# Fourth up unit of each MLP by seven quarter products, and x scaled by g and b on GpSimd

## What is computed

```python
def sq_relu_mlp(h, w_up, w_down):
    return jnp.square(jax.nn.relu(h @ w_up)) @ w_down
...
    xl = layer_norm(ALPHA * xl + ml[2] * dl, p["ln1_g"], p["ln1_b"])
    fl = sq_relu_mlp(modulate(xl, ml[3], ml[4]), p["w_up"], p["w_down"])
    xl = layer_norm(ALPHA * xl + ml[5] * fl, p["ln2_g"], p["ln2_b"])
```

## Time and profile before

| | |
|---|---|
| median of 3 runs | 1445.81 us (1445.0 to 1446.02) |
| span of the profiled execution, first to last instruction | 1442.8 us |
| difference of that span to the median | 3.0 us |
| TensorE busy | 1397.0 us, 97% of the span |
| VectorE busy | 1040.2 us, 72% |
| ScalarE busy | 543.1 us, 38% |
| GpSimd busy | 77.3 us, 5% |
| chain that ended last | TensorE 79%, VectorE 10%, ScalarE 5% |

### The profile page before, as it was taken

One profiled execution on the slowest core, in us unless ns is written; L12 is line 12 of the kernel. 1 busy time (PEld: TensorE's weight loads), 2 busy tenths in 40 slices (PEclk: granted clock), 3 DMA queues, 4 the chain that ended last, 5 costly groups with the idle time before them and its releaser, 6 DMA issues.

```text
span 1442.8 us, 22837 instructions
## 1 busy us (share of the span) xinstructions
PE 1397.0 (97%) x8806; PEld 1240.1 (86%) x8806; DVE 1040.2 (72%) x1651; ACT 543.1 (38%) x982; POOL 77.3 (5%) x146
## 2 busy tenths in 40 slices
PE   4999999999999999999999999999999999999996
PEld 3899988766779998998899879888999889989985
DVE  3694566777568876776776796877887677667778
ACT  4333343367454332332232254434443223223322
POOL 1300000010201000000000111001000000000011
PEclk9999999999999999999999999999999999999998
DMA  9701234696713312321221723551332122123141
GB/s 316 232 30 60 88 118 133 213 310 228 265 45 137 126 59 83 94 87 59 87 88 58 268 88 114 185 185 37 146 103 85 62 88 88 59 87 116 59 160 73
DMA packets 132300, 177.47 MB, mean 123 GB/s; under 512 B 4170, under 2 KB 104258, under 8 KB 131698
## 3 DMA queue, kind: packets, MB, share of 16 engines
q1 hardware_dynamic: 123250, 146.46, 31.4%
q0 software_dynamic: 7376, 26.76, 5.3%
q10 hardware_dynamic: 1584, 3.01, 0.6%
HBM read 166.94 MB, written 9.27 MB: 122 GB/s over the span
## 4 chain that ended last, share of the span: by engine, by line
PE 79%; DVE 10%; ACT 5%; issue 2%; DMA 2%; SPq 1%; POOL 0%; ACTq 0%; DVEq 0%
PE ps L801 40%; PE ps L1325 20%; PE ps L783 5%; PE ps L792 4%; PE ps L832 2%; DVE convT L2024 2%; PE ps L1133 2%; DVE wlo L1926 1%; ACT h_full L1722 1%; SPq L570 1%; DVE p_pad L2691 1%; DMA raw_more<-in_w_mod_l 1%; ACT tmp L1722 1%; ACT whi L1430 1%; PE ps L1144 1%
## 5 line engine op out<-in xcount | busy, mean ns | idle before, releaser
L1430 ACT ACTIVATE whi<-raw 128x512 fp32r<-128x512 f32 (+2 forms) x193 | 178.6, 935 | 357.8 <-PE ps L801 293.6
L801 PE MATMUL ps<-whi,hid_hi 128*128 128x512 f32 x640 | 249.6, 390 | 0.0
L801 PE MATMUL ps<-wlo,hid_hi 128*128 128x512 f32 x640 | 249.2, 389 | 0.0
L801 PE MATMUL ps<-whi,hid_lo 128*128 128x512 f32 x640 | 249.1, 389 | 0.0
L1926 DVE TENSOR_TENSOR wlo<-raw,whi 128x512 fp32r<-128x512 f32 (+2 forms) x193 | 204.9, 1070 | 26.0 <-ACT whi L1430 22.5
L2357 DVE TENSOR_TENSOR acc<-acc,ps 128x512 f32<-128x512 f32 x120 | 80.2, 684 | 122.0 <-PE ps L801 122.0
L801 PE MATMUL ps<-whi,h_hi 128*128 128x256 f32 (+1 forms) x480 | 157.4, 328 | 2.5 <-DVE wlo L1926 1.4
L801 PE MATMUL ps<-whi,h_lo 128*128 128x256 f32 (+1 forms) x480 | 152.9, 319 | 0.0
L801 PE MATMUL ps<-wlo,h_hi 128*128 128x256 f32 (+1 forms) x480 | 152.8, 318 | 0.0
L801 PEld LDWEIGHTS ps<-whi,hid_hi 128*128 128x128 f32 x640 | 120.1, 188 | 25.4 <-DVE wlo L1926 0.8
L801 PEld LDWEIGHTS ps<-whi,hid_lo 128*128 128x128 f32 x640 | 120.1, 188 | 25.1
(11 more groups left out here) (339 smaller groups left out, 2654.6 us busy)
## 6 DMA issues: line engine op xcount, KB each, us to landing
raw<-in_w_up_l SPq DMA_DIRECT2D x32, 1024.0 KB, 5.6
raw<-in_w_down_l SPq DMA_DIRECT2D x32, 1024.0 KB, 4.9
raw<-in_w_mod_l SPq DMA_DIRECT2D x26, 1024.0 KB, 5.8
raw<-in_w_in_l SPq DMA_DIRECT2D x12, 1024.0 KB, 5.2
raw_split<-in_w_mod_l SPq DMA_DIRECT2D x8, 1024.0 KB, 6.7
raw<-in_w_out_l SPq DMA_DIRECT2D x6, 1024.0 KB, 5.9
x_spill<-x_tok POOLq DMA_DIRECT2D x10, 512.0 KB, 2.9
x_tok<-x_spill POOLq DMA_DIRECT2D x10, 512.0 KB, 6.2
```

The costliest lines, as they stand in the source:

```text
L801: mm = pe.matmul(out, a_of(still, k), w_of(part, k), start=(first and k == 0 and part == 0 and still == 0), stop=(last and k == nk - 1 and ...
L1430: act.activation(ring_piece(whi, w, g), piece(w, g), ACT.Copy).then_inc(hi_done, 1)
```

## The change

`SU` goes from 4 to 3, so the fourth up unit (up 3) of each MLP is done by seven products. Its token sums, weight sums, high and low parts come forward by one up unit and two down units. The halves of `whi` and `wlo` are counted by `half(w)`, so that down 0 again takes the pieces that the unit of seven has left. The scaling of x by g and b leaves VectorE: GpSimd does it in `spill_x`, ahead of each tile's store. VectorE waits for all five tiles (`ln_x`) ahead of the weight sums of up 3.

```diff
-        SU, NS_UP, CONV_UP = 4, 12, 8
+        SU, NS_UP, CONV_UP = 3, 13, 6
...
-        PAR = [w % 2 for w in W_UP]
+
+        def half(w):
+
+            return (w + sum(w > u + SU for u in W_UP)) % 2
+
+        PAR = [half(w + SU) for w in W_UP]
...
             def spill_x(layer):
 
                 for t in range(NT):
+                    pool.wait_ge(ln_tr, 2 * NT * layer + t + 1)
+                    if t == 0:
+                        pool.wait_ge(gb_ld, 32 * (2 * layer + 1))
+                    pool.tensor_tensor(x[:, t, :], x[:, t, :], gb[:, 0, :], ALU.mult).then_inc(ss_, 1)
+                    steps[0] += 1
+                    pool.wait_ge(ss_, steps[0])
+                    pool.tensor_tensor(x[:, t, :], x[:, t, :], gb[:, 1, :], ALU.add).then_inc(ln_x, 1)
                     pool.wait_ge(ln_x, 2 * NT * layer + t + 1)
                     pool.dma_start(A["x_spill"][t * P:(t + 1) * P, :], x[:, t, :]).then_inc(x_re, 16)
...
-                    if u == SU and item == 0:
-                        pe.wait_ge(relu_ok[layer], 8 * (layer + 1))
+                    if u == SU and item in (0, 2):
+                        pe.wait_ge(relu_ok[layer], 2 * SU * (layer + 1) - (1 if item == 0 else 0))
...
                     if n < SU:
-                        split_hi(w + 1)
+                        split_hi(w + 1, None, (0, 1, 2))
                         relu_square(layer, 2 * n)
-                        if n == 3:
-                            for m, (k0, hf) in enumerate(((4, 1), (0, 0), (0, 1), (4, 0))):
-                                high_t(layer, m, k0, hf)
+                        for m, (k0, hf) in enumerate(((4, 1), (0, 0), (0, 1), (4, 0))):
+                            high_t(layer, m, k0, hf)
                         relu_square(layer, 2 * n + 1)
+                        split_hi(w + 1, None, (3, 4, 5))
                         continue
...
                     first_low(layer, f, hf)
                     if n == 5:
                         split_lo(W_UP[layer] + 2)
-                    if n >= 4:
-                        rescale(2 * layer, n - 4)
+                token_sums(layer)
...
                     if kind == "up":
-                        split_lo(w + 1)
+                        dve.wait_ge(ln_x, NT * (2 * layer + 1))
+                        weight_sums(w + 1)
+                        split_lo(w + 1, None, (0, 1, 2))
                         square_low(layer, 2 * n)
-                        if n == 2:
-                            rescale(2 * layer, 4)
-                        else:
-                            low_t(layer, 0, 4, 1, tlo[:, 0])
-                            low_t(layer, 1, 0, 0, tlo[:, 1])
+                        low_t(layer, 0, 4, 1, tlo[:, 0])
+                        low_t(layer, 1, 0, 0, tlo[:, 1])
                         square_low(layer, 2 * n + 1)
-                        if n == 2:
-                            token_sums(layer)
-                        else:
-                            low_t(layer, 2, 0, 1, hhi[:, 0:4, HALF:TOK])
-                            low_t(layer, 3, 4, 0, hlo[:, 0:4, HALF:TOK])
-                            dve.wait_ge(t_lo, 4 * (layer + 1))
+                        low_t(layer, 2, 0, 1, hhi[:, 0:4, HALF:TOK])
+                        split_lo(w + 1, None, (3, 4, 5))
+                        low_t(layer, 3, 4, 0, hlo[:, 0:4, HALF:TOK])
+                        dve.wait_ge(t_lo, 4 * (layer + 1))
                         continue
```

More of the change, by code:

```diff
@@ L437, in ring @@
                 return [[(n + 4 * PAR[layer]) % 8 for n in its] for its in PIECES]
-            r = [4 * (w % 2) + n for n in range(4)]
+            r = [4 * half(w) + n for n in range(4)]
             if w in W_OUT:
@@ L806, in w_cols @@
             def w_cols(w, row, lo, n):
-                return lambda part, k: WP[part][:, w % 2, k * row + lo:k * row + lo + n]
+                return lambda part, k: WP[part][:, half(w), k * row + lo:k * row + lo + n]
             def h_cols(buf, k0=0):
@@ L1345, in up @@
                         n = 2 * u + m
-                        pe.wait_ge(relu_ok[layer], 8 * layer + n - 1)
+                        pe.wait_ge(relu_ok[layer], 2 * SU * layer + n - 1)
                         b = 2 * (n % 2)
@@ L1746, in first_relu @@
                 cols = slice(hf * HALF, (hf + 1) * HALF)
-                c = (8 if hf else 4) * layer + n + 1
+                c = (2 * SU if hf else 4) * layer + n + 1
                 act.wait_ge(up_mm if hf else half_mm, (UPS if hf else 8) * layer + n + 1)
@@ L1761, in relu_square @@
                 act.activation(r.rearrange("p (b n) -> p b n", b=2), two(2 * (n % 2)), ACT.Relu).then_inc(relu_ok[layer], 1)
-                act.wait_ge(relu_ok[layer], 8 * layer + n + 1)
+                act.wait_ge(relu_ok[layer], 2 * SU * layer + n + 1)
                 act.activation(uhi[:, n, :], r, ACT.Square).then_inc(sq_hi, 1)
@@ L2483, in low_t @@
                 dve.wait_ge(t_hi, 4 * layer + n + 1)
-                if n == 0:
-                    dve.wait_ge(ln_x, NT * (2 * layer + 1))
                 if n == 2:
```

## The result

The changed kernel takes **1470.32 us** (median of 4 runs, 1469.95 to 1471.28) against 1445.4 us for the kernel before beside it (4 runs, 1443.83 to 1446.02): ratio 1.0176, 95% interval 1.0164 to 1.0188. It is slower by 24.9 us; 1472.0 with 1447 to 1482 was predicted. The profiled execution of the changed kernel took 1469.95 us, span 1468.1 us.

What follows compares the result with a forecast made beforehand. TensorE, busy 97% of the span, was taken as the bound. Per MLP 12.5 + 2.2 - 1.76 = 13 us, 26 for both, on 1442.8 gave 1468.8; with 3.0 around the span, 1472 us, range 1447 to 1482.

Steps and rivals of the forecast that it cites:

- The saving: Up 3 by seven products takes 12.32 us instead of 14.08: 1.76 us saved per MLP, 3.5 us for both.
- Duration on GpSimd: Each of ten two-input operations over 128x1024 takes 2.25 us, range 1.8 to 2.7; unheld, they end at 467 us.
- Turns: Wide GpSimd operations and VectorE's two-input operations or casts exclude each other for their whole length; chance 0.70.
- rivals without a hold: GpSimd and VectorE do not hold each other; only the queue ahead of up 3 costs: 1447.4 us, chance 0.11.
- with a hold on one side: GpSimd waits for VectorE's two-input operations, but they do not wait for it: 1450.7 us, chance 0.12.
- (a): VectorE's cast and subtraction chain to the last `h_lo`, held by GpSimd: TensorE's last four half units begin 5.6 us late.
- (b): Up 2 waits for its weights' low part behind held VectorE operations until 476.0 us: 12.5 us lost in all, (a) included.
- (c): Queue of token sums, weight sums and ScalarE work ahead of up 3: third low sum late, 2.2 us of waits.
- The sum: Loss per MLP: 12.5 + 2.2 - 1.76 = 13 us, for both 26 us.

Runs made afterwards that it cites:

- one-input: Changed kernel with GpSimd's ten operations replaced by ten over the same tile that read one SBUF input instead of two: 1460.38 us, ratio 1.0104.
- memset kernels: Changed kernel with GpSimd's ten operations replaced by ten that only write constants to the same tile: 1452.05 us, ratio 1.0054.
- the halves: Changed kernel with each of GpSimd's ten operations cut into two of 512 columns, same arithmetic: 1473.79 us, ratio 1.0203.

## Why the prediction was right, step by step

- **The saving.** 14.08 to 12.32 us in up 3, and 84 matmuls, exactly as counted.
- **Duration on GpSimd**, 2.25 us taken: 2.40 us alone, and 2.5 to 2.7 with the wait for VectorE in it. The tiles took 5.9 to 6.1 us each (start to start), with a gap of 0.30 us ahead of each spill that was not counted. The last addition ended at 469.8 us, 470.7 on the scale of the kernel before, against 467. The 2.25 was the middle of two ways to add up streams, and the runs bear out neither: a read and a write together took 1.06 us, hardly more than the write alone (0.97), and the second read added 1.34 us where 0.86 had been taken.
- **Turns.** Shown in both directions: GpSimd's operations alone cost 28.0 us, VectorE's held instructions end one working time behind GpSimd's, and the kernel without them has none of it. The rivals without a hold or with a hold on one side (1447.4 and 1450.7) are out. What the one-input and memset kernels add is that the hold depends on what GpSimd reads.
- **(a) The chain without slack:** 5.6 us foreseen, 5.15 measured (453.27 + 0.89 = 454.16 against 449.01); TensorE's wait 5.4 where 5.8 was said.
- **(b) Up 2 waits for its weights' low part:** 12.5 us in all foreseen (its terms give 476.0 - 463.32 = 12.7), 11.85 measured. Six of the twelve small operations were held, as counted. But the wait is 4.1 us (5.0 in the second MLP) and not 7, since the half units before it had already lost 2.65 us to the clock: 5.15 + 2.65 + 4.05 = 11.85. The time at which the weights are split is set by VectorE alone, so the slower TensorE cost nothing here.
- **(c) The queue behind it:** the term that was wrong. 2.2 us of waits in up 3 were foreseen; there are none in the first MLP and one of 0.3 us in the second. In their place up 2 took 2.65 us longer at the lower clock, a term that the prediction did not have, and this gave the queue the time that it lacked: VectorE had the third low sum at 494.16 + 1.49 = 495.65 us, TensorE's first matmul with it began at 496.28, and 2.65 us earlier it would have waited for 2.0. The queue itself was late as counted: without GpSimd's part TensorE waited 1.9 us for that same sum.
- **The sum:** 11.85 + 2.65 - 1.76 = 12.74 us for the first MLP against 13 foreseen. That it is so close is in part luck: the missing term, the clock (2.65 us), took nearly the place of the term that it hid (2.2 us). Where nothing hid it, in the kernel without the scaling, the count was 2.3 us short.

## What to carry to other kernels

Before work is moved from VectorE to GpSimd, ask which of VectorE's operations will run beside it, not whether GpSimd is idle: each two-input operation or cast of VectorE that met one of GpSimd's waited for its end, up to 2.4 us, here with no slack behind it, and twelve matmuls saved elsewhere (1.76 us) could not pay for that. Look first for gaps of VectorE itself (two of 2.9 us were enough for two of five pairs) and for ScalarE, which was busy 37 to 38%. Where TensorE is made to wait some microseconds, count the slower matmuls behind the wait as well, and ask whether a later wait hides them.

## What was not expected of the hardware

- **The clock after a wait.** TensorE worked at the 1.2 GHz level after waits of 5.4 and 4.1 us (2.65 us lost each time), after one of 4.9 us (29.97 - 28.16 = 1.8 us lost), after one of 3.7 us (15.86 - 14.33 = 1.5 us lost) and after some waits of 1.9 us and not after others, of one execution even (8.81 against 7.49 us for the same 48 matmuls). What is lost does not follow the length of the wait alone. In the change the clock had fallen before the wait for `h_lo` was over (0.65 in the mean from 452 to 453 us, 0.50 from 453 on). In the kernel with the one-input operations it fell only after the wait was over and a few matmuls had run at full rate:

```profile
453.21 0.31 PE L804 MATMUL ps<-h_hi,whi 128*128 128x320 f32 x1
...
453.75 0.47 PE L804 MATMUL ps<-h_hi,whi 128*128 128x320 f32 x1
```

- **GpSimd's time goes with the number of its SBUF inputs:** over 128x1024, 0.97 us for a memset, 1.06 us with one input, 2.40 us with two.
- **A turn can hold two GpSimd instructions** that follow each other directly (3.87 us for a subtraction of 1.23).
- **The start of a row does not tell whose turn it is.** VectorE's subtraction at 458.70 in the change began 0.13 us before GpSimd's multiplication at 458.83, and the one at 448.28 with the halves 0.28 us before GpSimd's at 448.56; both times VectorE was the one held.
